# Gate pieces inside the first attention, joined in pairs at fewer places of a step

## The chip, the cores and the metric

The kernel runs on one core of one Trainium2 chip. The metric is the device time of one execution in microseconds. In all views TensorE is PE, its weight loads PEld, VectorE DVE, ScalarE ACT, GpSimd POOL and SyncE SP.

## The reference, cut to what matters

Two transformer blocks run one after the other on 512 tokens of width 1024, in float32. The first block is the one that matters here:

```python
h = rms_norm(x, g_attn[l])
z = h @ w_in[l]
(fq, fk, fv, f_logit, nq, kc, vc, ksl, vsl, kwn, vwn, n_gate, g_a, g_b) = jnp.split(z, offsets, axis=-1)
o_fox = fox_attention(...)      # 8 heads of 64, causal, with a forget bias
o_nsa = nsa_attention(...)      # 8 heads, each a sum of compressed, selected and window attention
merged = jax.nn.sigmoid(g_a) * (o_fox @ w_br_fox[l]) + jax.nn.sigmoid(g_b) * (o_nsa @ w_br_nsa[l])
```

`g_a` and `g_b` are the gates of the two branches: 2048 of the columns of `z`. They are needed only after both attentions, so their matmuls can be run at any time before that.

## The kernel before

**Split operands.** Every large float32 product is made of three matmuls on rounded operands: weights high by activations high, high by low, low by high. ScalarE rounds a weight panel to its high part (`w_hi`, L580 `panel_hi`), VectorE subtracts to get the low part (`w_lo`, L1033 `panel_lo`). A panel is 1024 by 128; a ring of four panel slots is filled by SyncE, and a panel's two parts are made two panels ahead. A panel is eight pieces (k = 0 to 7), a piece three matmuls of 512 columns.

**The first attention.** `inst` lists 32 head instances: eight fox heads, then for each of eight NSA heads a compressed, a selected and a window instance. TensorE's program is written out by hand, software-pipelined over steps s = 0 to 33. In step s it makes the scores of instance s (`qk`, four query tiles t), turns the normalized probabilities of instance s - 2 by transposes (`turn_p`, j = 0 to 3; a compressed instance has one turn of four small transposes), and multiplies them by values (`pv`). Between these calls stand six places, numbered 0 to 5, where `gate_fill(s, slot)` puts a piece of a gate panel if the table `GATE_FILL` has one:

```python
            qk(s, 0)
            qk(s, 1)
            gate_fill(s, 0)
            turn_p(s - 2, 0)
            qk(s, 2)
            gate_fill(s, 1)
            qk(s, 3)
            turn_p(s - 2, 1)
            gate_fill(s, 2)
            pv(s - 2, 0)
            turn_p(s - 2, 2)
            gate_fill(s, 3)
```

Then come `pv(s - 2, 1)`, `turn_p(s - 2, 3)`, place 4, `pv(s - 2, 2)`, place 5 and `pv(s - 2, 3)`.

**The other engines.** VectorE in step s adds the bias to each score tile and takes the row maximum (`score`, L1185), subtracts the high part of each turned tile (`lo_turn`, `pt_lo`, L1219), normalizes instance s - 1 (`normalize`, `factor` L1200 and L1204, then four multiplications, L1210), and at a head's end adds and splits the output (L1235, L1227). ScalarE takes the exponentials (L690), the high part of each turned tile (`pt_hi`, L701), and in fox steps writes the next head's bias into the score buffer (L681). Transposes of instance s - 2 wait for `normed`; product j waits for `pt_lo`; the third score tile of a step waits until VectorE has read the first, since they share a bank.

**Where gate panels end.** All gate panels sum into one bank, `ps[:, 3, :]`. When a panel's last piece is done, VectorE moves it out, scaled, to `gate_z` (`gate_out`, L1244), at the position in its program that belongs to the place (`gate_at`); the next panel's first piece waits for that. The table therefore skips the place after a panel's end. At the end of a step in which a panel ended, ScalarE and VectorE split the panel two ahead (L580, L1033). For gate panels 0 to 7 `gate_out` also waits until the fox keys of a pair are used, since `gate_z` lies over them.

After step 33 the next stage, `branch`, starts on TensorE (L1673) when the last output is split.

## Time and profile before

| | |
|---|---|
| median of 3 runs | 1880.15 us (1878.94 to 1881.78) |
| the profiled execution's own time | 1880.16 us |
| its span in the profile | 1878.3 us |
| TensorE busy, share of the span | 1689.5 us, 90% |
| VectorE busy | 1156.5 us, 62% |
| ScalarE busy | 730.4 us, 39% |
| granted TensorE clock, mean | 0.951 |
| 183 to 424 us: TensorE busy | 215.59 us of 241 |
| 183 to 424 us: VectorE busy | 187.65 us of 241 |

The span is cut into 40 slices of 47 us. The first attention lies in slices 5 to 9. A row of a timeline has start, duration, engine, line, operation, output tile and input tiles, and in brackets how long the engine sat idle before it and what released it. Matmuls are pipelined: a matmul's duration reaches past the start of the next one, so what a matmul costs in a stream is the distance between starts.

### The profile page before, as it was taken

To read this page: it belongs to the slowest core of one execution; us is meant where nothing else is said; L and a number is where in the kernel's file an instruction comes from. 1 tells how busy PE (TensorE), PEld (TensorE's weight loads), DVE (VectorE), ACT (ScalarE), POOL (GpSimd) and SP (SyncE) were. 2 spreads that over 40 slices of the span, in tenths; PEclk is the share of its full clock that TensorE was granted. 3 is DMA by queue.
4 is the path that set the end of the run, shared out by engine and by line. 5 is a ranking of instruction groups with operands and counts; after the bars stand their busy time and mean duration, and the time that the engine had idled before them with its cause. 6 is when DMAs were issued, how large, how long until landed. Compare 5 with 4: busy or idle time off the path is not lost.

```text
span 1878.3 us, 22026 instructions
## 1 busy us (share of the span) xinstructions
PE 1689.5 (90%) x7666; PEld 1354.9 (72%) x7666; DVE 1156.5 (62%) x1741; ACT 730.4 (39%) x1216; POOL 142.5 (8%) x162
## 2 busy tenths in 40 slices
PE   7978889998999999998688867989889699999995
PEld 5867666667888888886566636778667488888884
DVE  6465688875575647465544686768865644354345
ACT  5244775654432323232242234543232344233232
POOL 0001400000000000002000880000000000000000
PEclk9988999998999999998599888999999899999998
DMA  4236821112444444443021110002222123232232
GB/s 154 93 104 185 162 64 46 53 46 76 170 159 166 159 165 160 165 160 131 0 80 55 45 45 0 1 19 94 79 78 90 56 91 100 91 99 95 96 100 79
DMA packets 46983, 178.98 MB, mean 95 GB/s; under 512 B 6256, under 2 KB 6512, under 8 KB 44608
## 3 DMA queue, kind: packets, MB, share of 16 engines
q1 hardware_dynamic: 38304, 136.75, 22.3%
q0 software_dynamic: 8608, 41.29, 7.3%
q8 instruction: 43, 0.70, 0.2%
q14 instruction: 28, 0.23, 0.0%
HBM read 168.04 MB, written 4.73 MB: 92 GB/s over the span
## 4 chain that ended last, share of the span: by engine, by line
PE 63%; DVE 19%; ACT 4%; issue 4%; DVEq 1%; ACTq 0%
PE ps L1673 17%; PE ps L1675 17%; PE ps L1674 17%; DVE conv L1559 3%; PE ps L1939 1%; DVE rstd L1497 1%; PE ps L1876 1%; DVE pt_lo L1522 1%; PE ps L1877 1%; PE ps L1878 1%; PE ps L1837 1%; DVE sq_acc L965 1%; ACT pt_hi L870 1%; DVE w_lo L954 1%; PE ps L1862 1%
## 5 line engine op out<-in xcount | busy, mean ns | idle before, releaser
L1673 PE MATMUL ps<-h_hi,w_hi 128*128 128x512 f32 x1216 | 488.6, 402 | 55.8 <-DVE h_lo L990 15.3
L1674 PE MATMUL ps<-h_lo,w_hi 128*128 128x512 f32 x1216 | 479.1, 394 | 0.0
L1675 PE MATMUL ps<-h_hi,w_lo 128*128 128x512 f32 x1216 | 479.0, 394 | 0.0
L1673 PEld LDWEIGHTS ps<-h_hi,w_hi 128*128 128x128 f32 x1216 | 232.2, 191 | 121.2 <-issue 30.5
L954 DVE TENSOR_TENSOR w_lo<-raw,w_hi 128x1024 fp32r<-128x1024 f32 x196 | 243.5, 1242 | 81.5 <-ACT w_hi L528 69.6
L528 ACT ACTIVATE w_hi<-raw 128x1024 fp32r<-128x1024 f32 x189 | 198.3, 1052 | 238.2 <-DMA raw<-in_panels 236.9
L1674 PEld LDWEIGHTS ps<-h_lo,w_hi 128*128 128x128 f32 x1216 | 232.2, 191 | 49.3 <-issue 2.7
L1675 PEld LDWEIGHTS ps<-h_hi,w_lo 128*128 128x128 f32 x1216 | 231.6, 190 | 49.4
L1673 PE MATMUL ps<-f_hi,w_hi 128*128 128x512 f32 x432 | 171.0, 396 | 0.0
L1675 PE MATMUL ps<-f_hi,w_lo 128*128 128x512 f32 x432 | 170.6, 395 | 0.0
L1674 PE MATMUL ps<-f_lo,w_hi 128*128 128x512 f32 x432 | 170.6, 395 | 0.0
L1673 PEld LDWEIGHTS ps<-f_hi,w_hi 128*128 128x128 f32 x432 | 81.1, 188 | 19.9 <-issue 0.2
L1674 PEld LDWEIGHTS ps<-f_lo,w_hi 128*128 128x128 f32 x432 | 81.1, 188 | 19.8 <-issue 0.2
L1675 PEld LDWEIGHTS ps<-f_hi,w_lo 128*128 128x128 f32 x432 | 81.1, 188 | 19.7
L1033 DVE TENSOR_TENSOR w_lo<-raw,w_hi 128x1024 fp32r<-128x1024 f32 x54 | 65.8, 1221 | 32.5 <-ACT w_hi L580 26.7
L1331 DVE SCALAR_TENSOR_TENSOR X<-ps,mod,X 128x512 f32 (+1 forms) x32 | 24.0, 750 | 98.9 <-PE ps L1675 98.9
L1559 DVE SCALAR_TENSOR_TENSOR conv<-u_pad,vec,conv x96 | 72.1, 751 | 14.4 <-DVE conv L1559 14.4
L701 ACT ACTIVATE pt_hi<-ps 128x512 fp32r<-128x512 f32 (+4 forms) x104 | 46.3, 446 | 73.5 <-PE ps L1837 72.7
L1219 DVE TENSOR_TENSOR pt_lo<-ps,pt_hi 128x512 fp32r<-128x512 f32 (+4 forms) x104 | 52.0, 503 | 34.9 <-ACT pt_hi L701 34.5
L580 ACT ACTIVATE w_hi<-raw 128x1024 fp32r<-128x1024 f32 x61 | 63.7, 1049 | 10.9 <-DMA raw<-in_panels 10.6
L774 ACT ACTIVATE tmp_v<-tmp_s 128x512 f32<-128x512 f32 x32 | 20.2, 633 | 116.2 <-DVE tmp_s L1379 116.2
L1876 PE MATMUL ps<-h_hi,w_hi 128*128 128x512 f32 x128 | 57.0, 445 | 5.7 <-DVE gate_z L1244 5.7
(361 smaller groups left out, 2665.0 us busy)
## 6 DMA issues: line engine op xcount, KB each, us to landing
raw<-in_panels SPq DMA_DIRECT2D x252, 512.0 KB, 3.5
wm<-in_w_mod POOLq DMA_DIRECT2D x16, 1536.0 KB, 10.1
scratch_r<-r POOLq DMA_DIRECT2D x8, 320.0 KB, 9.3
X<-in_x SPq DMA_DIRECT2D x4, 512.0 KB, 7.3
bias<-scratch_c POOLq DMA_DIRECT2D x8, 256.0 KB, 8.9
kd<-k_hi POOLq DMA_DIRECT2D x16, 128.0 KB, 3.6
kd<-k_lo POOLq DMA_DIRECT2D x16, 128.0 KB, 5.2
bias<-scratch_r POOLq DMA_DIRECT2D x8, 256.0 KB, 3.0
```

What stands on the lines that cost most here:

```text
L528: act.activation(w_hi[:, slot], raw[:, slot], ACT.Copy).then_inc(hi_ready, 1)
L580: act.activation(w_hi[:, n % RING], raw[:, n % RING], ACT.Copy).then_inc(hi_ready, 1)
L701: act.activation(pt_hi[0:rows, at:at + w], ps[0:rows, 4 + r % 2, 0:w], ACT.Copy).then_inc(sem("pt_hi_done"), 1)
L954: dve.tensor_tensor(w_lo[:, slot], raw[:, slot], w_hi[:, slot].bitcast(F32), ALU.subtract).then_inc(lo_ready, 1)
L1033: dve.tensor_tensor(w_lo[:, n % RING], raw[:, n % RING], w_hi[:, n % RING].bitcast(F32), ALU.subtract)\
L1219: dve.tensor_tensor(pt_lo[0:rows, at:at + w], ps[0:rows, 4 + r % 2, 0:w], pt_hi[0:rows, at:at + w].bitcast(F32), ALU.subtract).then_inc(se ...
L1331: dve.scalar_tensor_tensor(x, ps[:, u % 2:u % 2 + 1, :], mod[:, bass.ds(i * RING + (gain + u), 1)], x, ALU.mult, ALU.add).then_inc(bank_fr ...
L1559: dve.scalar_tensor_tensor(conv[:, bass.ds(i, 1), :], u_pad[:, bass.ds(i, 1), tap:tap + T], vec[:, bass.ds(i * TAPS + (V_AT["dw_w"] + tap) ...
L1673: pe.matmul(out, w_hi[:, u, b, :], hi[:, k, :N], start=start, stop=False)
L1674: pe.matmul(out, w_hi[:, u, b, :], lo[:, k, :N], start=False, stop=False)
L1675: ins = pe.matmul(out, w_lo[:, u, b, :], hi[:, k, :N], start=False, stop=stop)
L1876: pe.matmul(ps[:, 3, :], hi, h_hi[:, k, :], start=k == 0, stop=False, skip_group_check=True)
```

## The change

`gate_slots` lists fewer places, and each place in `GATE_FILL` now holds two pieces, k and k + 1 of the same panel, run one after the other. The rule that the place after a panel's end is skipped stays, but a place is now two pieces. `gate_fill` loops over the pieces of its place.

```diff
     def gate_slots(s):
 
         if s < 2:
-            return (0, 1, 2, 3, 4, 5)
+            return (0, 2, 3)
         if s >= NI:
-            return (0, 2, 3, 5) if is_big(s - 2) else (0, 2)
+            return (2, 3) if is_big(s - 2) else (2,)
         if is_big(s) and is_big(s - 2):
-            return (0, 1, 2, 3, 5)
-        return (0, 2, 3, 5) if is_big(s - 2) else (0, 1, 2)
+            return (0, 2, 3)
+        return (2, 3) if is_big(s - 2) else (0, 1)
...
             elif _at < 16 * KT:
-                GATE_FILL[s, n] = divmod(_at, KT)
-                _at += 1
+                GATE_FILL[s, n] = [divmod(_at, KT), divmod(_at + 1, KT)]
+                _at += 2
...
-            g, k = GATE_FILL[s, slot]
-            n = BASE["gate"] + g
-            if k == 0:
-                pe.wait_ge(lo_ready, n + 1)
-                pe.wait_ge(bank_free, n + 2)
...
+            for g, k in GATE_FILL[s, slot]:
+                n = BASE["gate"] + g
+                if k == 0:
+                    pe.wait_ge(lo_ready, n + 1)
+                    pe.wait_ge(bank_free, n + 2)
```

What the table says, per kind of step (without the skipped places):

| step s, turned instance s - 2 | before | now |
|---|---|---|
| 0 and 1 | places 0 to 5, one piece | 0, 2, 3, two pieces each |
| fox or selected, large | 0, 1, 2, 3, 5 | 0, 2, 3 |
| window, compressed | 0, 1, 2 | 0, 1 |
| compressed, large | 0, 2, 3, 5 | 2, 3 |
| 32 and 33 | 0, 2, 3, 5 | 2, 3 |

With the skips, the pieces in steps 0 to 2 are 6, 5, 5 before and 6, 4, 6 now; in steps 3 to 8 they are 4, 4, 5, 4, 5, 3 before and 4, 4, 6, 4, 6, 2 now; steps 9 to 31 hold 82 before and 86 now; steps 32 and 33 hold 5 before and none now. Panels end in steps 1, 2, 4, 6, 8, 10, 12, 15, 17, 19, 21, 24, 26, 28, 30, 33 before and in 1, 2, 4, 6, 7, 9, 12, 14, 16, 18, 20, 22, 24, 27, 29, 31 now. Place 5 held a piece in steps 3, 5, 6, 7, 8 and, between 9 and 29, in twelve more; now in none.

**TensorE, step 13 (window), third and fourth scores** (`kn_hi`, `kn_lo` are the keys, `nqs` the queries). Before:

```order
L1817 MATMUL ps<-kn_hi_70,nqs 128x384
L1818 MATMUL ps<-kn_lo_74,nqs 128x384
L1876 MATMUL ps<-h_hi,w_hi 128x512
L1877 MATMUL ps<-h_lo,w_hi 128x512
L1878 MATMUL ps<-h_hi,w_lo 128x512
L1817 MATMUL ps<-kn_hi_70,nqs 128x512
L1818 MATMUL ps<-kn_lo_74,nqs 128x512
L1876 MATMUL ps<-h_hi,w_hi 128x512
L1877 MATMUL ps<-h_lo,w_hi 128x512
L1878 MATMUL ps<-h_hi,w_lo 128x512
```

Now:

```order
L1817 MATMUL ps<-kn_hi_70,nqs 128x384
L1818 MATMUL ps<-kn_lo_74,nqs 128x384
L1876 MATMUL ps<-h_hi,w_hi 128x512
L1877 MATMUL ps<-h_lo,w_hi 128x512
L1878 MATMUL ps<-h_hi,w_lo 128x512
L1876 MATMUL ps<-h_hi,w_hi 128x512
L1877 MATMUL ps<-h_lo,w_hi 128x512
L1878 MATMUL ps<-h_hi,w_lo 128x512
L1817 MATMUL ps<-kn_hi_70,nqs 128x512
L1818 MATMUL ps<-kn_lo_74,nqs 128x512
```

Two pieces stand between the scores in place of one, and the piece behind the fourth score is gone.

**TensorE, from step 13 into step 14 (compressed): products with compressed values `vcs`, first compressed scores, transposes of the selected probabilities `sb`.** Before:

```order
L1862 MATMUL ps<-pt_hi,vcs 128x512
L1863 MATMUL ps<-pt_lo,vcs 128x512
L1817 MATMUL ps<-kc_hi,nqs 128x8
L1818 MATMUL ps<-kc_lo,nqs 128x8
L1817 MATMUL ps<-kc_hi,nqs 128x16
L1818 MATMUL ps<-kc_lo,nqs 128x16
L1876 MATMUL ps<-h_hi,w_hi 128x512
L1877 MATMUL ps<-h_lo,w_hi 128x512
L1878 MATMUL ps<-h_hi,w_lo 128x512
L1837 MATMUL ps<-cst,sb_81 128x128 x4
```

Now:

```order
L1862 MATMUL ps<-pt_hi,vcs 128x512
L1863 MATMUL ps<-pt_lo,vcs 128x512
L1817 MATMUL ps<-kc_hi,nqs 128x8
L1818 MATMUL ps<-kc_lo,nqs 128x8
L1817 MATMUL ps<-kc_hi,nqs 128x16
L1818 MATMUL ps<-kc_lo,nqs 128x16
L1837 MATMUL ps<-cst,sb_81 128x128 x4
```

The piece between the scores and the transposes is gone.

**TensorE, end of step 14: the last transposes and products.** Before:

```order
L1837 MATMUL ps<-cst,sb_81 128x128
L1862 MATMUL ps<-pt_hi,vns 128x256
L1863 MATMUL ps<-pt_lo,vns 128x256
L1876 MATMUL ps<-h_hi,w_hi 128x512
L1877 MATMUL ps<-h_lo,w_hi 128x512
L1878 MATMUL ps<-h_hi,w_lo 128x512
L1862 MATMUL ps<-pt_hi,vns 128x128
L1863 MATMUL ps<-pt_lo,vns 128x128
```

Now:

```order
L1837 MATMUL ps<-cst,sb_81 128x128
L1862 MATMUL ps<-pt_hi,vns 128x256
L1863 MATMUL ps<-pt_lo,vns 128x256
L1862 MATMUL ps<-pt_hi,vns 128x128
L1863 MATMUL ps<-pt_lo,vns 128x128
```

The piece ahead of the last product, at place 5, is gone.

**VectorE, step 1, the scores and the evacuation of the first gate panel:**

```order
 L1185 ISA sb_81,row_max<-ps,sb_81 128x256
 L1185 ISA row_max 128x1
+L1244 TENSOR_TENSOR gate_z_120<-ps,rs_98 128x512
 L1185 ISA sb_81,row_max<-ps,sb_81 128x384
 L1185 ISA row_max 128x1
```

The evacuation now stands ahead of the two large scores; before it stood behind them.

## Rows read from the trace of the kernel before

**Rows 1.** Who waited for whom, 183 to 424 us: us in total, times, longest.

```profile
PE ps L1817 <- DVE row_max L1185: 7.5, 12, 1.3
...
PE ps L1862 <- DVE pt_lo L1219: 6.7, 15, 1.0
...
PE ps L1876 <- DVE gate_z L1244: 5.7, 6, 1.9
```

**Rows 2.** Groups by line and shape, 183 to 424 us, VectorE: busy us, mean ns, idle before.

```profile
L1033 DVE TENSOR_TENSOR w_lo<-raw,w_hi 128x1024 fp32r<-128x1024 f32 x15 | 18.3, 1217 | 0.0
...
L1244 DVE TENSOR_TENSOR gate_z<-ps,rs 128x512 f32<-128x512 f32 x16 | 10.9, 682 | 0.4 <-PE ps L1878 0.4
```

**Rows 3.** Timeline of TensorE, first matmuls of steps 3, 9, 12, 14, 15: start, us.

```profile
208.65 0.27 PE L1817 MATMUL ps<-kd,qs 128*128 128x128 f32 x1
...
259.67 0.27 PE L1817 MATMUL ps<-kn_hi,nqs 128*128 128x128 f32 x1
...
280.83 0.27 PE L1817 MATMUL ps<-kn_hi,nqs 128*128 128x128 f32 x1
...
293.41 0.27 PE L1817 MATMUL ps<-kc_hi,nqs 128*128 128x8 f32 x1
...
300.07 0.27 PE L1817 MATMUL ps<-kn_hi,nqs 128*128 128x128 f32 x1
```

**Rows 4.** Timeline of TensorE, steps 1 and 5; in brackets the idle time before.

```profile
197.43 0.58 PE L1876 MATMUL ps<-h_hi,w_hi 128*128 128x512 f32 x1 [1.87 <-DVE gate_z L1244]
197.81 0.63 PE L1877 MATMUL ps<-h_lo,w_hi 128*128 128x512 f32 x1
198.24 0.63 PE L1878 MATMUL ps<-h_hi,w_lo 128*128 128x512 f32 x1
...
229.24 0.45 PE L1817 MATMUL ps<-kd,qs 128*128 128x384 f32 x1 [1.26 <-DVE row_max L1185]
```

**Rows 5.** Timeline of TensorE, step 12, what follows transposes.

```profile
282.54 0.42 PE L1817 MATMUL ps<-kn_hi,nqs 128*128 128x384 f32 x1
282.80 0.34 PE L1818 MATMUL ps<-kn_lo,nqs 128*128 128x384 f32 x1
...
284.37 0.47 PE L1876 MATMUL ps<-h_hi,w_hi 128*128 128x512 f32 x1
284.69 0.39 PE L1877 MATMUL ps<-h_lo,w_hi 128*128 128x512 f32 x1
```

**Rows 6.** Timeline of TensorE, end of step 12, step 13, start of 14.

```profile
287.85 0.33 PE L1862 MATMUL ps<-pt_hi,vns 128*128 128x128 f32 x1 [0.42 <-DVE pt_lo L1219]
...
289.33 0.60 PE L1834 MATMUL ps<-cst,p_cmp 128*32 128x128 f32 x4
290.35 0.44 PE L1817 MATMUL ps<-kn_hi,nqs 128*128 128x384 f32 x1 [0.42 <-DVE row_max L1185]
...
293.88 0.48 PE L1876 MATMUL ps<-h_hi,w_hi 128*128 128x512 f32 x1
...
294.76 0.66 PE L1837 MATMUL ps<-cst,sb 128*128 128x128 f32 x4
```

**Rows 7.** Timeline of VectorE, step 13.

```profile
291.16 0.67 DVE L1219 TENSOR_TENSOR pt_lo<-ps,pt_hi 32x512 fp32r<-32x512 f32 x1
...
292.23 0.67 DVE L1185 CUSTOM_DVE_ANT_0 sb<-ps,bias 128x512 f32<-128x512 f32 x1
...
293.43 1.27 DVE L1210 TENSOR_SCALAR sb<-sb,factor 128x128 f32<-128x128 f32 x4
```

**Rows 8.** Timeline of TensorE, end of step 14.

```profile
299.17 0.39 PE L1876 MATMUL ps<-h_hi,w_hi 128*128 128x512 f32 x1
...
299.87 0.25 PE L1862 MATMUL ps<-pt_hi,vns 128*128 128x128 f32 x1
```

**Rows 9.** Timeline of TensorE, step 32 and the next stage.

```profile
415.37 0.98 PE L1837 MATMUL ps<-cst,sb 128*128 128x128 f32 x7 [0.39 <-DVE sb L1210]
...
430.81 0.76 PE L1673 MATMUL ps<-qs,w_hi 128*128 128x512 f32 x1 [3.58 <-DVE nqs L1227]
```

More of the change, by code:

```diff
@@ L1869, in gate_fill @@
                 return
-            g, k = GATE_FILL[s, slot]
-            n = BASE["gate"] + g
-            if k == 0:
-                pe.wait_ge(lo_ready, n + 1)
-                pe.wait_ge(bank_free, n + 2)
-            hi, lo = w_hi[:, n % RING, k, :], w_lo[:, n % RING, k, :]
-            pe.matmul(ps[:, 3, :], hi, h_hi[:, k, :], start=k == 0, stop=False, skip_group_check=True)
-            pe.matmul(ps[:, 3, :], hi, h_lo[:, k, :], start=False, stop=False, skip_group_check=True)
-            ins = pe.matmul(ps[:, 3, :], lo, h_hi[:, k, :], start=False, stop=k == KT - 1, skip_group_check=True)
-            if k == KT - 1:
-                ins.then_inc(used, 1)
+            for g, k in GATE_FILL[s, slot]:
[3 more added lines that the diff above has]
+                    pe.wait_ge(bank_free, n + 2)
+                hi, lo = w_hi[:, n % RING, k, :], w_lo[:, n % RING, k, :]
+                pe.matmul(ps[:, 3, :], hi, h_hi[:, k, :], start=k == 0, stop=False, skip_group_check=True)
+                pe.matmul(ps[:, 3, :], hi, h_lo[:, k, :], start=False, stop=False, skip_group_check=True)
+                ins = pe.matmul(ps[:, 3, :], lo, h_hi[:, k, :], start=False, stop=k == KT - 1, skip_group_check=True)
+                if k == KT - 1:
+                    ins.then_inc(used, 1)
         pe.wait_ge(setup, 3)
```

2 lines of the change are left out of this document (1 added, 1 removed).

## The prediction

> **What bounds the kernel now.** I read the 40 slices first: the change touches one stretch, 183 to 431 us, and everything outside it keeps its instructions and their order. Inside, the table of waits [rows 1] shows TensorE stopping for VectorE in three ways: for the release of a score bank (7.5 us in 12 waits), for the low part of a turned probability tile (6.7 us in 15), and, at the first matmul of a gate panel, for the evacuation of the last panel (5.7 us in 6). Then I read the timelines of TensorE and VectorE step by step. Both engines are nearly full there and release each other in turn, so what counts is not the sum of work but which of them is ahead at each hand-over. The same 384 gate matmuls run in both kernels. A gate piece is three matmuls and takes 0.70 us between its neighbours (299.17 to 299.87) [rows 8], a pair 1.40 us. So the time changes only by the waits that pieces cover or leave bare, and by the slow clock.
>
> I call a step by what it scores: fox (0 to 7), then in turn compressed (8, 11, ...), selected (9, 12, ...), window (10, 13, ...). What a step turns and multiplies by values is the step two before.
>
> **1. Start, up to step 3.** Before, TensorE waits 1.87 us at 197.43 for gate_z, which stands on VectorE behind both large scores, and its next matmuls start 0.43 us apart (197.81, 198.24) [rows 4], where the warm ones of a piece take 0.70 us for three [rows 8]: the clock fell to the lower level, 1.2 GHz, after the wait. Now gate_z stands ahead of the two large scores, but for panel 0 it still waits until all keys of fox head 1 are used, so I halve the wait: -0.95. One piece fewer follows it, at 3 x 0.43: -1.3. Step 2 has one piece more, +0.70, and at its end gate_z (0.68) [rows 2] goes ahead of the last low part, where it lies beside ScalarE: -0.65. Sum **-2.2**; bounds -4 (no wait and no slow matmuls) and 0.
>
> **2. Steps 3 to 8,** 51.0 us (208.65 to 259.67) [rows 3]. One piece more: +0.70. The new cost is place 5, the piece between the last two products with values. The last product needs the last turned tile to go through ScalarE and VectorE. With a piece in the gap nothing waits: 299.17, then 299.87 on time [rows 8]. Where the old plan skipped place 5, TensorE stood idle for 0.42 us at 287.85 [rows 6]; with the end of the earlier matmul counted as streamed I take 0.55. Five of these steps had place 5 filled: +2.75. Against it, the pair at place 0 covers 0.70 more of the wait before the third score in steps 5 and 7, of which 1.26 us at 229.24 is the largest [rows 4]: -1.2. Sum **+2.2**; bounds -1 (ScalarE sets the pace of fox steps and hides all) and +4.
>
> **3. Steps 9 to 32, up to the transposes of step 32,** 155.7 us (259.67 to 415.37) [rows 3, 9]. I build it from the read triple 12 to 14, 280.83 to 300.07, 19.24 us with 11 pieces [rows 3].
> With all places full it now has 14 pieces: +2.10.
> The wait at 290.35 (0.42 idle, 0.67 from the end of streaming) goes, since the pair at place 0 outlasts the split w_lo (1.22 us) [rows 2, 6]: -0.67. The pair at place 2 covers another 0.2 before a first product.
> The place-5 wait, paid once in this triple (287.85), is now paid twice: +0.58.
> The large term is the compressed step. Its first transposes need the normalized tile. In step 13 the order is: compressed transposes from 289.33, pt_lo at 291.16, the largest score at 292.23, normalizing at 293.43 for 1.27, transposes at 294.76 [rows 6, 7]: 2.53 us from largest score to transposes, which no piece can shorten. Three things used to fill TensorE meanwhile: pieces at places 1 and 2 of the window step and place 0 of the compressed one (293.88). Now one pair, at place 1, which stands before the fourth score. TensorE has 0.70 us less to do, and the matmuls of the largest score end 0.70 later after those transposes; of that I let VectorE's own queue ahead of it (pt_lo and the third score) hide 0.15, so the largest score starts 0.55 late. So a wait of about 0.1 becomes 1.4: +1.30.
> Full triple: 19.24 + 2.10 - 0.87 + 0.58 + 1.30 = 22.35. Steps 9 to 31 are eight selected, eight window and seven compressed steps: eight triples less one compressed step (8.3, by the same walk), plus the 1.4 of step 32: 8 x 22.35 - 8.3 + 1.4 = 171.9. That holds 108 pieces; the plan puts 86 there, because eleven pairs are skipped for evacuations: 22 x 0.70 = -15.4. A skipped pair bares what it covered. By the walk that is 0.1 to 0.5 where place 2 or 3 of a selected or place 3 of a compressed step is skipped, 1.0 at place 0 of a window step behind w_lo, and 1.5 to 2.1 where gate_z falls ahead of the normalizing of a compressed turn (steps 16, 22, 31). Mean 0.8, eleven times: +8.8. Result 165.3, so **+9.6**. Of this 4 x 0.70 = 2.8 is pieces that step 9 to 31 take over from the last steps. Bounds: if the compressed wait stayed at 0.1 and no hole cost anything, 165.3 - 8.8 - 10.4 = 146.1, -9.6; if each hole cost the full 2.1, +24. I take the walk, which is nearest to the read triple.
>
> **4. Tail,** 415.37 to 430.81 [rows 9]. Five pieces lay here, all beside waits; taking them out saves nothing. But gate_z (0.68) and one w_lo (1.22) [rows 2] leave VectorE's last chain, of which the first counts whole and the second for what stands behind ScalarE's copy: **-1.1**, bounds -1.9 and 0.
>
> Nothing else moves: DMA issues keep their order on both queues; kd and bias loads follow the score steps. The joined piece should cost nothing by itself. After transposes the next matmul starts late: 284.37 to 284.69 is 0.32 where a streamed one takes 0.23. But the score matmul of 384 columns behind transposes shows the same, 282.54 to 282.80, 0.26 [rows 5], so the loss moves with the transposes and is not saved. The Trainium skill (TensorE: Matmul & The Clock Gate, step-by-step on LDWEIGHTS) says that the next weights load while the current matmul runs, which speaks for long runs; by that alone each of 64 joins would gain. The trace prices such a join at most 0.08, 5.1 us in all, and shows it paid elsewhere.
>
> Sum: -2.2 + 2.2 + 9.6 - 1.1 = +8.5. On the profiled execution's own 1880.16 us, which is the median of the runs shown (1880.15) to 0.01, this gives 1888.7; I say **1889**.
>
> **Rivals.** *Faster.* The covers win: the score and evacuation waits (7.5 + 5.7) go, and the compressed steps do not get a longer wait, because VectorE, no longer held by TensorE's late transposes, runs ahead by as much as the pair is long. It decides at one point: the transposes of the compressed steps start less than 0.5 us after TensorE is ready. Place 5 still costs 0.42 in 18 steps, 7.6. 1880.2 - 13.2 + 7.6 = 1874.6. For it: the read waits are real, and VectorE idles where TensorE is busy. Against: the 2.53 us chain in [rows 7] has no gap in it.
> *No change.* VectorE's own work per triple is unchanged, and if it is the true pace the loss at place 0 is given back at the next hand-over: +9.6 shrinks to about +2, 1881.
> *Worse.* The boundaries (gate_z 0.68 and w_lo 1.22, fifteen times [rows 2]) stay as exposed as now instead of lying under pairs: another 0.5 each, 7.5, 1896. The long waits of steps 17 and 32 could also bring the low clock, as at 197.43; if nine matmuls then run at 0.43 instead of 0.23, that is 1.8 us more each time. The Trainium skill (same page, what's actually happening) says that activity releases the throttle; the granted clock after 197.43 agrees.
> *The joins pay.* Rule above, with place 5 and holes as walked: 1889 - 5.1 = 1883.6.
>
> **How the numbers follow.** The runs shown lie within 0.15% of each other, and I call 0.2% (3.8 us) what can be told from no change: 1876.4 to 1883.9. Chances: forecast (1884 to 1893) 0.53, faster 0.16, no change 0.13, worse 0.14, joins 0.04. Slower by over 0.2%: 0.53 + 0.14 = 0.67; within 0.2%: 0.13 + 0.04 = 0.17; faster 0.16. The range 1876 to 1898 leaves out the faster case and the far end of the worse one, nearly 0.2. The forecast's own range is 1884 to 1893.
>
> **What would show it.** After: no TensorE wait for gate_z, or under 1.5 us in all; the waits for the score bank about halved; the waits of the last product for pt_lo at almost every step, some 20 times 0.4; the waits of compressed-step transposes for the normalized tile at 1.2 to 1.5 us eight times, some 10 us; step 9 starting within 1 us of 259.7; the next stage starting about 8 us later than 430.8. I am wrong if step 9 starts several us earlier, or if transposes in compressed steps wait under 0.5 us.

## The result, and the profile after

| | before | after |
|---|---|---|
| median | 1880.91 us (1878.94 to 1881.78, 4 runs) | 1912.38 us (1907.90 to 1916.11, 4 runs) |
| the profiled execution's own time | 1880.16 us | 1915.98 us |
| its span in the profile | 1878.3 us | 1914.2 us |
| mean granted TensorE clock | 0.951 | 0.938 |

The change makes the kernel slower by 31.5 us, a ratio of 1.0168 (95% interval 1.0137 to 1.0198). 1889 us was forecast, with 1898 as the upper end. The direction was right; the loss is almost four times the 8.5 us forecast.

I read the windows first, cut at the same instructions in both kernels: the stage from its first waiting matmul to the first matmul of `branch`. Columns: stretch, its length, busy time of PE, PEld, DVE, ACT and POOL (with instructions), granted clock, share of DMA, GB/s. Before:

```profile
181.12:430.81 249.69, 220.32 (x1164) 170.04 (x1165) 193.12 (x651) 159.09 (x444) 24.98 (x46) 0.96 0.32 77
259.67:415.37 155.70, 141.53 (x753) 107.38 (x753) 128.50 (x463) 94.34 (x285) 3.95 (x7) 0.99 0.15 49
```

After, the whole stage, and steps 9 to 32 up to the transposes of step 32:

```profile
182.69:461.34 278.65, 234.94 (x1165) 186.40 (x1165) 193.63 (x651) 158.79 (x444) 25.04 (x46) 0.90 0.30 69
263.34:444.68 181.34, 153.92 (x763) 121.42 (x762) 129.64 (x465) 94.89 (x286) 3.95 (x7) 0.92 0.14 45
```

The stage takes 278.65 us for 249.69, 29.0 more. VectorE and ScalarE do the same work in the same busy time. TensorE runs the same matmuls (1164 and 1165 records), but is busy 14.6 us longer (220.32 to 234.94), and idle 14.3 us longer (29.37 to 43.71). **Half of the loss is waiting, half is matmuls at a lower clock**: the granted clock of the stage falls from 0.96 to 0.90. Of the rest of this execution's 35.8 us, 1.57 lie ahead of the stage and 5.4 in later stages (1452.9 for 1447.5 us), whose instructions did not change; another run of the same table of pieces (e10 below) has 1447.5 there, so these 5.4 are no part of the change.

The other executions say the same. Each has its own mean granted clock on record: 0.943 and 0.942 for the changed kernel's executions of 1907.9 and 1908.8 us, 0.939 and 0.938 for those of 1916.1 and 1916.0. Their mean is 0.9405, that of the 68 executions of the kernel before that were timed beside the experiments 0.9515. Within either kernel an execution is longer by 1.7 or 1.8 us for each 0.001 of clock that it has less, over all kernels of this case by 1.5. The 0.011 between the two is then worth, by estimate, 16 to 20 us of the 31.5; the rest is waiting.

The waits, after, which answer to [rows 1] (waiting line, what it waited for, us in total, times, longest):

```profile
PE ps L1862 <- DVE pt_lo L1219: 17.3, 32, 2.0
PE ps L1837 <- DVE sb L1210: 16.1, 12, 2.7
PE ps L1817 <- DVE row_max L1185: 5.2, 9, 1.3
...
PE ps L1876 <- DVE gate_z L1244: 1.3, 1, 1.3
```

The waits for gate_z are nearly gone, as meant (5.7 in six before, 1.3 in one now). Those for the score bank went from 7.5 to 5.2. In their place, waits of products for `pt_lo` (6.7 in 15 before) and of first transposes for the normalized tile grew to 33.4 us in 44. Eighteen of the former stand ahead of a step's last product with nothing at place 5, seventeen of them 0.45 or 0.46 us long and one 0.26. The latter, in steps that score a compressed tile, look like this, here in step 20 (columns: start, duration, engine, line, operation, output and inputs, form, count, idle time before it and what ended it):

```profile
350.70 0.66 PE L1837 MATMUL ps<-cst,sb 128*128 128x128 f32 x4 [1.38 <-DVE sb L1210]
...
352.18 0.39 PE L1877 MATMUL ps<-h_lo,w_hi 128*128 128x512 f32 x1
```

Five such waits are 1.38 us. Where a panel ends in the window step ahead, the wait is longer. VectorE and TensorE at the end of step 16 and in step 17:

```profile
322.95 0.68 DVE L1219 TENSOR_TENSOR pt_lo<-ps,pt_hi 32x512 fp32r<-32x512 f32 x1 [1.02 <-ACT pt_hi L701]
323.56 0.67 DVE L1244 TENSOR_TENSOR gate_z<-ps,rs 128x512 f32<-128x512 f32 x1
324.16 0.54 DVE L1185 CUSTOM_DVE_ANT_0 sb<-ps,bias 128x384 f32<-128x384 f32 x1
...
324.63 0.67 DVE L1185 CUSTOM_DVE_ANT_0 sb<-ps,bias 128x512 f32<-128x512 f32 x1
...
325.83 1.27 DVE L1210 TENSOR_SCALAR sb<-sb,factor 128x128 f32<-128x128 f32 x4
```

```profile
323.78 0.47 PE L1862 MATMUL ps<-pt_hi,vcs 32*128 32x512 f32 x1 [0.67 <-DVE pt_lo L1219]
...
327.16 1.11 PE L1837 MATMUL ps<-cst,sb 128*128 128x128 f32 x4 [2.14 <-DVE sb L1210]
...
329.91 0.63 PE L1877 MATMUL ps<-h_lo,w_hi 128*128 128x512 f32 x1
```

`gate_z` (323.56) stands in VectorE's chain from pt_lo to the normalizing, and the chain has no gap; TensorE meanwhile has no piece to run, since the place behind a panel's end is skipped, and stands 2.14 us. After that a gate matmul takes 0.43 us to its neighbour where at 352.18 it takes 0.23: the lower level of 1.2 GHz. Step 10 shows the two losses side by side:

```profile
274.67 0.61 PE L1817 MATMUL ps<-kn_hi,nqs 128*128 128x384 f32 x1 [1.32 <-DVE row_max L1185]
...
275.39 0.63 PE L1876 MATMUL ps<-h_hi,w_hi 128*128 128x512 f32 x1
...
277.52 0.63 PE L1878 MATMUL ps<-h_hi,w_lo 128*128 128x512 f32 x1
```

```profile
278.74 0.69 DVE L1185 CUSTOM_DVE_ANT_0 sb<-ps,bias 128x512 f32<-128x512 f32 x1 [1.87 <-PE ps L1818]
...
279.95 1.27 DVE L1210 TENSOR_SCALAR sb<-sb,factor 128x128 f32<-128x128 f32 x4
```

```profile
281.28 0.33 PE L1837 MATMUL ps<-cst,sb 128*128 128x128 f32 x1 [1.38 <-DVE sb L1210]
```

A wait of 1.32 us for the score bank; then the pair at place 1 runs at 1.2 GHz, 2.56 us (275.39 to 277.95) for 1.40; VectorE waits 1.87 us for the largest score behind it; the normalizing begins at 279.95; the transposes wait 1.38 us. VectorE is late by what TensorE is late, so nothing of the slow pair is won back. It does not make the next wait longer either: behind window step 19, which ran at the full clock, the transposes of step 20 wait the same 1.38 us.

### The profile page after: what moved, and what is told of

Read it like the earlier page. It is cut to its first block, busy times and chain, and to the rows that moved or that the text cites. A ratio compares the mean times of both kernels' runs of the same rounds, so it can differ in the third digit from the quotient of the medians.

```text
span 1914.2 us, 22026 instructions
## 1 busy us (share of the span) xinstructions
PE 1710.5 (89%) x7666; PEld 1376.4 (72%) x7666; DVE 1157.4 (60%) x1741; ACT 730.4 (38%) x1216; POOL 143.6 (8%) x162
## 4 chain that ended last, share of the span: by engine, by line
PE 63%; DVE 18%; ACT 5%; issue 4%; DVEq 1%; ACTq 0%
PE ps L1673 17%; PE ps L1674 16%; PE ps L1675 16%; DVE conv L1559 3%; PE ps L1876 2%; PE ps L1878 1%; PE ps L1877 1%; PE ps L1939 1%; DVE rstd L1497 1%; PE ps L1837 1%; DVE pt_lo L1522 1%; DVE sb L1210 1%; DVE sq_acc L965 1%; PE ps L1862 1%; DVE w_lo L954 1%
## 5 line engine op out<-in xcount | busy, mean ns | idle before, releaser
L1673 PE MATMUL ps<-h_hi,w_hi 128*128 128x512 f32 x1216 | 491.6, 404 | 54.8 <-DVE h_lo L990 15.5
L1033 DVE TENSOR_TENSOR w_lo<-raw,w_hi 128x1024 fp32r<-128x1024 f32 x54 | 65.8, 1221 | 31.5 <-ACT w_hi L580 25.8
L774 ACT ACTIVATE tmp_v<-tmp_s 128x512 f32<-128x512 f32 x32 | 20.3, 633 | 116.4 <-DVE tmp_s L1379 116.4
L1837 PE MATMUL ps<-cst,sb 128*128 128x128 f32 x240 | 46.9, 299 | 16.1 <-DVE sb L1210 16.1
```

The lines of the kernel that those rows point to most:

```text
L1033: dve.tensor_tensor(w_lo[:, n % RING], raw[:, n % RING], w_hi[:, n % RING].bitcast(F32), ALU.subtract)\
L1673: pe.matmul(out, w_hi[:, u, b, :], hi[:, k, :N], start=start, stop=False)
L1837: ins = pe.transpose(ps[:, 4 + r % 2, (t - j) * P:(t - j + 1) * P], sb[big_of[s]][:, SB_AT[t] + j * P:SB_AT[t] + (j + 1) * P], ident)
```

## The experiments

Every run was timed against the kernel before on the same chip; ratios are to it, with 95% intervals. The kernel before had medians of 1880.5 (e1 to e4), 1880.5 (e5 to e8), 1881.0 (e9 to e12) and 1883.0 us (e13 to e15) beside them; the numbers are those of the runs' labels, given with each heading. In the diffs (place, pieces) is an entry of the table. "Busy" and "idle" are TensorE's in the stage of one profiled execution, to be read beside 220.32 and 29.37 us in the kernel before and 234.94 and 43.71 in the changed one.

### Undoing one part at a time

**e2: Place 5 filled again.** In the changed kernel, half of the pair at place 3 goes to place 5:

```diff
+        three = ((3, 1), (5, 1))
...
-            return (0, 2, 3)
-        return (2, 3) if is_big(s - 2) else (0, 1)
+            return ((0, 2), (2, 2), *three)
+        return ((2, 2), *three) if is_big(s - 2) else ((0, 2), (1, 2))
```

> The changed kernel with the pair at place 3 split into one piece at place 3 and one at place 5 (from step 2 on), otherwise paired as it is. Theory: a bare place 5 costs 0.46 to 0.58 us; about 18 of them are filled again, so 8 to 10 us go, and with less idle time some of the low clock: 1898 to 1904. Rival (the transposes of the compressed steps are the whole cause): the waits at place 5 only move to the next hand-over, 1909 to 1913.

Measured: 1904.45 us (1899.83 to 1909.16), ratio 1.0113 [1.0080, 1.0147], 7.9 us less than the changed kernel, the lower end of the 8 to 10 that the waits add up to. Of low clock nothing is gone: the mean clock of its four executions is that of the changed kernel, 0.9405. The rival (1909 to 1913) does not hold by the time. In the profiled execution, the longest of the four, the waits for `pt_lo` fell from 17.3 to 10.2 us and TensorE is idle for 5.7 us less (37.98); some of it did come back, in waits of first transposes (17.5 for 16.1 for the normalized tile). That profile has more low clock than the changed kernel's (busy 237.94), so its stage is only 2.7 us shorter.

**e3: The compressed steps covered.** The window steps' pair at place 1 moves to place 0 of the compressed steps:

```diff
-        return (2, 3) if is_big(s - 2) else (0, 1)
+        return (0, 2, 3) if is_big(s - 2) else (0,)
```

> The changed kernel with the pair at place 1 of the window steps (ahead of the fourth score) moved to place 0 of the steps that score a compressed tile (ahead of the transposes that wait 1.38 us). Theory: the largest score is 1.4 us earlier and a pair fills the wait, so 8 waits of 1.38 to 2.7 (14.1 us in the profile) fall under 0.3; with them goes the low clock that follows the longest: 12 us of waits and some 8 of slow matmuls, 1890 to 1896. Place 5 stays bare. Rival (VectorE's own chain sets the pace there, what one wait loses another gains): 1906 to 1912.

Measured: 1899.96 us (1896.99 to 1903.58), ratio 1.0104 [1.0075, 1.0133], 12.4 us less. The waits, up to the end of the stage:

```profile
PE ps L1862 <- DVE pt_lo L1219: 19.3, 38, 0.8
PE ps L1837 <- DVE sb L1210: 7.3, 7, 2.2
PE ps L1817 <- DVE row_max L1185: 5.8, 12, 0.7
```

Waits for the normalized tile fell from 16.1 us in 12 to 7.3 in 7. (The eight longest had added up to 13.7 us, not 14.1.) The waits gained less than forecast because the pair left place 1 of the window steps: with neither place 1 nor 2 filled the product of the compressed tile waits, as here in step 16,

```profile
316.48 0.46 PE L1862 MATMUL ps<-pt_hi,vcs 32*128 32x512 f32 x1 [0.79 <-DVE pt_lo L1219]
```

and where a panel ends in the window step, place 0 behind it is skipped and the full wait remains (2.15 us at 363.20, in step 23). So idle time fell by only 5.9 us (37.80), and busy time by 8.2 (226.70), the stage clock being 0.94 for 0.90. The larger part of this gain is clock, in the four executions too: their mean is 0.9465 for 0.9405, worth 9 to 11 of the 12.4 us by the estimate above.

**e14: Both at once.**

```diff
+        three = ((3, 1), (5, 1))
...
-            return (0, 2, 3)
-        return (2, 3) if is_big(s - 2) else (0, 1)
+            return ((0, 2), (2, 2), *three)
+        return ((0, 2), (2, 2), *three) if is_big(s - 2) else ((0, 2),)
```

> The changed kernel with both parts undone at once: place 5 filled with half of the pair of place 3, and the window steps' second pair moved to place 0 of the compressed steps. Alone they took 8 and 12.4 us off. Theory (separate waits, separate prices): together 20, 1892; what is left are the bare place 2 of the window steps (8 waits of 0.67 = 5.4), and that the pieces are used up by step 29, so the last steps have none. 1889 to 1895. Rival (both take off the same low clock): less than the sum, 1896 to 1900.

Measured: 1893.30 us (1892.49 to 1899.15), ratio 1.0056 [1.0040, 1.0071]. That is 19.1 us less than the changed kernel (21 by the ratios, as this chip ran the kernel before 2 us slower), for 7.9 + 12.4 = 20.3 alone. The two prices add up, and so does the idle time of the profiles: 5.7 and 5.9 us less alone, 10.5 together (33.24). That speaks for separate waits, but it is not a clean test. All three plans place other numbers of pieces per step than the changed kernel, so panels end elsewhere in them. In this one three panels end at place 0 of a window step; place 0 of the compressed step behind it is skipped, and waits of 2.14 or 2.15 us for the normalized tile are left in steps 14, 20 and 26, each with a low clock behind it (0.68 or 0.69 over the step). Of the 10 us that still separate this run from the kernel before, its executions' clock (0.942 for 0.951 on that chip) can make up all.

### The same question from the kernel before

**e12: One joining alone, place 5 to place 3**, in the fifteen steps that have both; order and panels stay:

```diff
+        if s >= 2 and (s, 3) in GATE_FILL and (s, 5) in GATE_FILL:
+            GATE_FILL[s, 3] = GATE_FILL[s, 3] + GATE_FILL.pop((s, 5))
```

> The kernel before with the other joining alone: the piece at place 5 stands at place 3 behind the one there, in the fifteen steps that have both, from step 2 on; nothing else moves. Theory: each place 5 left bare costs 0.46 to 0.58 us, and few of the waits are long enough to bring the low clock: +7 to +9, 1888 to 1890. Rival 1 (what place 5 loses, the pair at place 3 wins back): 1881 to 1883. Rival 2 (many short waits bring the low clock too): 1893 or more.

Measured: 1893.85 us (1889.48 to 1895.96), ratio 1.0071 [1.0058, 1.0085]. The profiled execution was the shortest, 1889.48, and in it the stage is only 7.5 us longer (257.14), at a clock of 0.98 (0.96 before):

```profile
182.75:439.89 257.14, 221.41 (x1164) 171.41 (x1165) 193.29 (x651) 159.14 (x444) 24.99 (x46) 0.98 0.31 75
```

```profile
303.42 0.33 PE L1868 MATMUL ps<-pt_hi,vns 128*128 128x128 f32 x1 [0.46 <-DVE pt_lo L1225]
```

The fifteen waits are 0.46 us each as expected; with the earlier matmul's end counted as streamed, 0.5 to 0.6. Of the profiled execution's 9.3 us, 7.5 lie in the stage and 1.6 ahead of it, where nothing was changed. Nor is it free of low clock: steps 3 and 20 ran at 0.84 and 0.83, where the kernel before has 1.00, and took 1.2 and 1.6 us more than there, while steps 0 and 1, the same in both, took 2.5 less. The median is 4.4 us above the profiled execution, and its number is rival 2's, not the theory's. The five executions' clocks go with their times: 0.953 for 1889.5 us, 0.950 and 0.951 for 1892.7 and 1893.9, 0.948 for 1895.7 and 1896.0. The next run asks whether the clock makes the difference.

**e15: The same with the wait filled**, by one gate matmul run twice:

```diff
+            if (s, 5) not in GATE_FILL and s >= 2 and is_big(s - 2):
+                repeat()
```

> The kernel before with the piece of place 5 joined to place 3, as run already (median 1893.9, profile 1889.5), with one gate matmul (512 columns, hi x hi of the last piece, while its panel is open) run again in each bare place 5: 0.23 us of work in a wait of 0.46. (The gate values are changed by the repeated products.) Theory: the waits' ends stay, 9.3 us; the low clock that came on top in the median (some 4 us) is less: 1889 to 1891. Rival 1 (the clock has no part in it): 1893 to 1894.5. Rival 2 (the repeated matmul delays the last product): 1896.

Measured: 1889.44 us (1888.04 to 1893.56) beside 1882.97, ratio 1.0040 [1.0025, 1.0055]; without the fill it was 1.0071 [1.0058, 1.0085]. The intervals do not touch. Step for step the profile has the same lengths as the run without the fill, within 0.1 us, so the fill moved no wait's end. About 0.3% went, and of what was tried only the clock accounts for it. The two profiles, both with a stage clock of 0.98, do not show it themselves, but the executions do: 0.951 to 0.954 here, 0.948 to 0.953 without the fill. The median is the theory's; the first rival would have left the ratio, the second raised it.

**e11: The other joining alone, place 1 to place 0**, in eleven fox and selected steps:

```diff
+        if s >= 2 and is_big(s) and is_big(s - 2) and (s, 0) in GATE_FILL and (s, 1) in GATE_FILL:
+            GATE_FILL[s, 0] = GATE_FILL[s, 0] + GATE_FILL.pop((s, 1))
```

> The kernel before with one joining alone: in fox and selected steps from step 2 on, the piece at place 1 stands at place 0 behind the one there (eleven pairs); number, order and panels of all pieces unchanged. Theory (pairs cost nothing, bare places do): place 1 has no wait to cover and the pair at place 0 outlasts some waits for the score bank, so 1878 to 1881. Rival (joining itself costs, say 0.5 us a pair): 1886.

Measured: 1880.22 us (1876.56 to 1882.62), ratio 0.9994 [0.9985, 1.0003]. A pair as such costs nothing that these runs can tell. This run and e12 both join pieces; e12 bares a wait by it and this one does not.

### Clock or wait

**e1: Small matmuls in the bare waits** of the changed kernel, n = 9 ahead of the transposes in compressed steps and 3 at place 5:

```diff
+        def idle_fill(n):
+            for _ in range(n):
+                pe.matmul(ps[:, 2, 3 * P:4 * P], cst_r[:, 0:P], cst_r[:, P:2 * P], start=True, stop=True,
+                          skip_group_check=True)
...
+            if kind_of(s) == "cmp" or s == NI:
+                idle_fill(9)
...
+            if is_big(s - 2) and s > 8:
+                idle_fill(3)
```

> The changed kernel with matmuls added that compute nothing that is used (9 of 128 columns before the first transposes of each step that scores a compressed tile, and of step 32; 3 before the last product with values, from step 9 on). They write a part of a score bank that nothing reads. At 0.11 us each they last 1.0 us in waits of 1.38 and 0.33 in waits of 0.46, so the waits' ends do not move. Theory (two factors, waits and the low clock they bring): the ends of the waits stay, but TensorE no longer stands idle, the granted clock of 264 to 448 us rises from 0.91 to 0.97 or more, and most of the 14.6 us by which the stage's matmuls run longer goes: 1898 to 1902. Rival (waits alone make the loss, the clock is a detail of one profile): 1912, or some us more for the added work, 1912 to 1916.

Measured: 1906.29 us (1899.40 to 1912.57), ratio 1.0122 [1.0079, 1.0164]. By the median 6 us less, but the interval overlaps that of the changed kernel. The profiled execution speaks against an effect: step 17 and the whole stretch are as before the fill,

```profile
322.69 0.47 PE L1862 MATMUL ps<-pt_hi,vcs 32*128 32x512 f32 x1 [0.67 <-DVE pt_lo L1219]
...
323.79 1.20 PE L1884 MATMUL ps<-cst_r 128*128 128x128 f32 x9
326.07 1.11 PE L1837 MATMUL ps<-cst,sb 128*128 128x128 f32 x4 [1.08 <-DVE sb L1210]
...
328.82 0.63 PE L1877 MATMUL ps<-h_lo,w_hi 128*128 128x512 f32 x1
```

```profile
262.24:443.73 181.49, 166.27 (x879) 134.72 (x879) 129.67 (x465) 94.92 (x286) 3.96 (x7) 0.92 0.14 45
324.00:325.00 1.00, 0.99 (x9) 0.85 (x8) 0.90 (x7) 0.95 (x3) 0.48 (x1) 0.98 0.00 0
325.00:326.00 1.00, 0.00 (x0) 0.00 (x0) 1.00 (x5) 0.75 (x4) 0.07 (x1) 0.50 0.42 53
```

181.49 us at a clock of 0.92 (181.34 and 0.92 in the changed kernel). TensorE ran without a gap from 323.79 to 324.99, and the clock fell right behind it: 0.98 in the slice up to 325, 0.50 in the next. In this execution the small matmuls did not keep the clock. But the profile was taken of one of two long executions (1911.2 and 1912.6 us, clock 0.942 and 0.941); the other two took 1899.4 and 1901.4 us at 0.949 and 0.948, a clock that none of the changed kernel's four reached (0.938 to 0.943), and their times are in the theory's range. So this run leaves open whether the small matmuls did something in half of the executions. Next come matmuls of a gate piece's size.

**e5: Gate-size matmuls in the same places:**

```diff
+                    pe.matmul(ps[:, 3, :], w_hi[:, (BASE["gate"] + g) % RING, k, :], h_hi[:, k, :],
+                              start=False, stop=False, skip_group_check=True)
...
+            if kind_of(s) == "cmp" or s == NI:
+                repeat(5)
...
+            if kind_of(s - 2) == "cmp":
+                repeat(2)
...
+            if is_big(s - 2) and s > 8:
+                repeat(1)
```

> The changed kernel with matmuls of a gate piece's own size (512 columns) in the bare places: the hi x hi matmul of the piece that ran last is run again, one ahead of the last product, two ahead of the first product that follows transposes of a compressed tile, five ahead of the transposes in steps that score a compressed tile, and in step 32. (While no gate panel is open, small matmuls that nothing reads stand in their place, none at the second of the three. The gate values come out changed by the repeated products; no other part differs.) They take 0.23, 0.46 and 1.15 us in waits of 0.46, 0.67 and 1.38 or more. Theory: the clock followed the full-size pieces that are missing there, so it stays up, and most of the 14.6 us of slower matmuls goes: 1898 to 1903, the waits' ends unmoved. Rival 1 (after the run with small matmuls): the low clock does not depend on these waits, the same stretches run slow, 1906 to 1912. Rival 2: added work is on the path: above 1912.

Measured: 1904.28 us (1902.80 to 1906.91), ratio 1.0109 [1.0072, 1.0146]; 8.1 us less than the changed kernel. In its profile:

```profile
181.12:449.81 268.69, 239.57 (x1264) 191.63 (x1265) 193.40 (x651) 158.72 (x444) 24.93 (x46) 0.95 0.30 71
260.05:432.65 172.60, 158.20 (x849) 125.67 (x848) 129.32 (x465) 94.88 (x285) 3.95 (x7) 0.98 0.14 47
```

```profile
317.50 1.31 PE L1875 MATMUL ps<-cst_r 128*128 128x128 f32 x10
319.79 0.80 PE L1837 MATMUL ps<-cst,sb 128*128 128x128 f32 x4 [0.98 <-DVE sb L1210]
...
322.22 0.63 PE L1890 MATMUL ps<-h_lo,w_hi 128*128 128x512 f32 x1
```

The stage takes 268.7 us, 10.0 less than in the changed kernel, though it runs 99 matmuls more; steps 9 to 32 take 172.60 for 181.34, and their clock is 0.98. The 8.7 us are clock, or nearly: at the full clock in both profiles, the fill makes window steps 13, 19 and 28 0.4 to 0.5 us longer and compressed steps 20 and 29 0.3 to 0.4 shorter, which nearly cancels. In steps 17 and 23, where no panel was open and small matmuls stood in again, the low clock stayed; in the others of steps 10 to 31 where the changed kernel's profile has it, it is gone. All four executions have a clock of 0.946 to 0.950, above all four of the changed kernel, and none of their times reaches the changed kernel's shortest. Beside e1 the time alone proves nothing (1904.3 and 1906.3 us); that matmuls of this size did more than small ones rests on the two profiles, steps 17 and 23 and the executions' clocks. The median shows less than the 9 to 14 us I had expected; this profile's later stages have 7.8 us more than the kernel before (1455.3 for 1447.5), as the changed kernel's profile has 5.4.

### Where in the stage, and the panels' ends

**e4: Pairs in steps 0 to 8 only** (old entries from step 9):

```diff
+        if s < 9:
+            if s < 2 or is_big(s):
+                return ((0, 2), (2, 2), (3, 2))
+            return ((2, 2), (3, 2))
```

> Pairs only in steps 0 to 8, the old single pieces and places from step 9 on. Theory by the sum on record: -2.2 at the start, +2.2 in steps 3 to 8, so 1881 within 2 us; as the trace of the changed kernel shows step 8 alone 2.4 us longer, up to 1883. Rival (pairs cost about the same in every step, 30 us over 32 steps): 1888.

Measured: 1887.57 us (1884.51 to 1892.32), ratio 1.0033 [1.0021, 1.0046], the rival's value. But the profile puts only 3.2 us ahead of step 9, and 7.6 behind it, where the entries are the old ones: by step 8 the pairs have placed one piece more, so that all later panels end one place sooner. And nearly all of these 10.8 us are slower matmuls, not waits: busy 230.60, idle 29.86, the stage clock 0.92 for 0.96. Two runs take this apart.

**e6: The same with one piece fewer in step 8**, so that nothing slips:

```diff
+        if s < 8:
+            return ((0, 2), (2, 2), (3, 2)) if s < 2 or is_big(s) else ((2, 2), (3, 2))
+        if s == 8:
+            return ((2, 2), (3, 1))
```

> As the run with pairs in steps 0 to 8 alone, with one piece fewer in step 8 (one at place 3, for two), so that from step 9 on every piece and every panel end stands exactly where the kernel before has it. Theory: in that run the 8.2 us that steps 9 to 30 took longer came from the panel ends, which one piece more had moved (steps 15 and 24 took 12.2 and 10.3 for 7.8); here they are back, so only the change of the first nine steps is left: 3 us longer by the start of step 9, 1882 to 1885. Rival (a slip of one piece costs nothing, the difference comes from another cause): 1887 to 1888 again.

**e7: The slip alone**, no pairs:

```diff
+        if s == 8:
+            return ((0, 1), (2, 1), (3, 1), (5, 2))
```

> The kernel before with one piece more in step 8 (two at place 5) and otherwise its own places: all later panel ends come one place earlier, nothing is paired. Theory: the place of the panel ends has a price of its own, about that of steps 9 to 30 in the run with pairs in steps 0 to 8: +8 in the profile less what the median gave, 1884 to 1889. Rival: 1881 within 2 us.

Measured: e6 1883.84 us (1881.62 to 1889.99), ratio 1.0011 [0.9995, 1.0028], and e7 1883.91 us (1882.30 to 1892.72), 1.0018 [0.9999, 1.0037]. Both medians lie over 3 us above the kernel before, near what the theories say, and together make about the 7 us of the run above; but neither interval excludes no change. In e6's profile the stage is 4.1 us longer, all of it busy time (224.45) at an unchanged idle time (29.34); steps 8, 9 and 20 ran at a low clock. So what e6 prices is where low clock fell, not waits. What the slip does to the waits is plain in e7's profile: step 15 takes 10.9 us for 7.8. A panel now ends at place 5 of step 14 and `gate_z` stands ahead of the normalizing; idle before matmuls in that step goes from 0.95 to 2.37 us, and the rest is low clock behind it (0.84 over the step, 1.00 before):

```profile
301.41 0.44 PE L1840 MATMUL ps<-cst,sb 128*128 128x128 f32 x2 [1.68 <-DVE sb L1213]
```

**e8: Old pieces in steps 0 to 8, pairs behind them:**

```diff
+        if s == 8:
+            return ((0, 1), (2, 1), (3, 1), (5, 2))
+        if s > 8:
...
+            if is_big(s) and is_big(s - 2):
+                return ((0, 2), (2, 2), (3, 2))
+            return ((2, 2), (3, 2)) if is_big(s - 2) else ((0, 2), (1, 2))
```

> Old places and single pieces in steps 0 to 8 (with the one piece more in step 8), pairs from step 9 on exactly as in the changed kernel. Theory: the loss lies here: the 25.6 us of steps 9 to 32 and the tail's 1.2 stay, the first nine steps' are back: 1906 to 1910. Rival (the early waits set off the later ones, without them the later steps run as walked, +9.6): 1888 to 1893.

Measured: 1905.96 us (1900.82 to 1912.31), ratio 1.0120 [1.0074, 1.0166]. It has the slip too, so 22 us stand against the run with the slip alone; in the profiles of the two, 13.0 us are busy time (235.12 for 222.11) and 11.0 idle (42.28 for 31.30). The loss lies from step 9 on; the rival's +9.6 is excluded.

**e10: gate_z off the chain.** In the changed kernel, in window steps:

```diff
-            gate_at(s, 0)
+            if kind_of(s) != "win":
+                gate_at(s, 0)
...
-            gate_at(s, 1)
+            if kind_of(s) != "win":
+                gate_at(s, 1)
...
             normalize(s - 1)
+            if kind_of(s) == "win":
+                gate_at(s, 0, 1)
```

> The changed kernel with one order of VectorE changed: in window steps the evacuation of a panel (gate_z, 0.67 us) stands behind the normalizing instead of ahead of the third score or behind the fourth. That is so in steps 16, 22, 25 or 31 where a panel ends at place 0 or 1. Theory: gate_z is on the chain to the transposes of the next step, so these waits (2.14 at step 17, 1.99 at step 23, 2.69 at step 32) fall by 0.5 to 0.7 each to the 1.38 of the other compressed steps, about 2 us, and the low clock behind them with it: 1904 to 1910. Rival (the chain there is ScalarE's, gate_z lies beside it): the waits stay within 0.2, 1912.

Measured: 1912.91 us (1912.75 to 1912.96, 3 runs), ratio 1.0169 [1.0153, 1.0185]. No gain, the rival's time; but not by its mechanism. The waits did fall, each by 0.6 (to 1.54, 1.38 and 2.09 us), and step 17 is 0.3 us shorter (11.34 for 11.67). In step 23 the next one grew by as much:

```profile
378.15 0.80 PE L1862 MATMUL ps<-pt_hi,vns 128*128 128x512 f32 x1 [1.35 <-DVE pt_lo L1219]
```

```profile
379.07 0.80 PE L1866 MATMUL ps<-pt_hi,vns 128*128 128x512 f32 x1 [1.95 <-DVE pt_lo L1219]
```

And the low clock came in places where the changed kernel, with the same waits, did not have it. Step 20 in this run, to be read beside 350.70 and 352.18 above:

```profile
350.28 1.12 PE L1841 MATMUL ps<-cst,sb 128*128 128x128 f32 x4 [1.39 <-DVE sb L1210]
...
353.03 0.63 PE L1881 MATMUL ps<-h_lo,w_hi 128*128 128x512 f32 x1
```

The same wait (1.39 and 1.38 us), the same instructions; here the matmuls are 0.43 apart and the step takes 11.21 us, there 0.23 and 8.28. Step 21 is the other way round, 8.96 us here at the full clock and 10.53 at 0.84 there, and the clocks of the three executions (0.939 each) are within those of the changed kernel.

### Using what costs nothing

**e9: Pairs in steps 0 to 3 only.** Both plans have placed 20 pieces by then, so nothing slips:

```diff
+        if s < 4:
+            return ((0, 2), (2, 2), (3, 2))
```

> The changed plan (pairs at places 0, 2, 3) in steps 0 to 3 only; from step 4 on every piece and panel end exactly as before. Both plans have placed 20 pieces by then, so nothing slips. Theory: from the first score to step 4 the kernel before took 36.0 us and the changed one 34.0; the later steps start from the same state, so 2 us less: 1878 to 1879.5. Rival: the gain is given back by the next steps (VectorE, whose work is the same, is no earlier): 1880 to 1882.

Measured: 1880.31 us (1878.32 to 1882.75), ratio 0.9999 [0.9990, 1.0008], the rival's value. In the profile the way to step 4 is 2.3 us shorter (33.7 for 36.0) and stays so to step 11 (87.9 for 90.2). Step 11 then takes 10.79 us for 8.62, at a low clock, behind the same waits (0.66 and 0.58 us, for 0.65 and 0.57).

**e13: This and place 1 joined to place 0:**

```diff
+        if s < 4:
+            return ((0, 2), (2, 2), (3, 2))
...
+        if s >= 4 and is_big(s) and is_big(s - 2) and (s, 0) in GATE_FILL and (s, 1) in GATE_FILL:
+            GATE_FILL[s, 0] = GATE_FILL[s, 0] + GATE_FILL.pop((s, 1))
```

> Both joinings that cost nothing alone: the changed plan in steps 0 to 3, and from step 4 on the piece of place 1 joined to place 0 in fox and selected steps; everything else as before. Theory: in the profiles the first shortened the way to step 4 by 2.0 us, the second that from step 9 to 31 by 1.3, and both medians lay 0.7 us under the kernel before; together 1878 to 1880 (-1 to -3). Rival: both gains are only where low-clock stretches happened to fall, 1881.

Measured: 1878.42 us (1876.58 to 1883.24, 11 runs) beside 1882.97 (15 runs), ratio 0.9979 [0.9969, 0.9988]. It is the only version that beats the kernel before, by 0.2%, and it beats the changed one. Its waits up to 424 us, against [rows 1]:

```profile
PE ps L1868 <- DVE pt_lo L1225: 8.9, 19, 1.1
PE ps L1882 <- DVE gate_z L1250: 5.2, 6, 1.3
PE ps L1823 <- DVE row_max L1191: 4.0, 10, 0.7
PE ps L1843 <- DVE sb L1216: 3.2, 8, 0.6
```

For the score bank 4.0 us, where it was 7.5.

## Why the prediction was right and wrong

**Term 1, start to step 3, -2.2: right.** From the first score to step 3 the profile gives 25.05 us for 26.68, -1.6; the wait for gate_z is 1.31 for 1.87. Pairs in steps 0 to 3 alone show it again (2.3 us by step 4).

**Term 2, steps 3 to 8, +2.2: low by 1.5, nearly all of it clock.** Measured 54.75 for 51.02, +3.7. Step 8 alone takes 9.62 for 7.26: a panel now ends at place 3 of step 7, its `gate_z` (252.33) and `w_lo` (254.70) stand ahead of step 8's scores on VectorE, and the first product of that step, at 258.29, waits 2.04 us where it waited 0.96. I had no row for that in this term. But step 8 also ran at a clock of 0.82; in e5's profile, with the same pieces (and small matmuls ahead of its transposes) and the full clock, it takes 8.32 us, and steps 3 to 8 together 53.44, +2.4. There the way from the first score to step 9 is 78.10 us for 77.70 before: terms 1 and 2, which add up to nothing, hold apart from the clock.

**Term 3, steps 9 to 32, +9.6: this step failed; it measured +25.6.** Its parts did not fail alike.

- *The full triple* held. Steps with all places filled and the full clock take 8.94 us (selected, steps 15 and 30), 5.28 (window, step 19) and 8.28 (compressed, step 20), 22.5 in all, where the walk had 22.35; selected steps 9 and 24, in which a panel ends at place 3, take 8.5. The wait of the first transposes was walked as 1.4 and measured 1.38; place 5 at 0.58 measured 0.46 of bare idle, and 7.9 us when filled again.
- *The clock* was missing from the sum, and is the larger part. 8.7 us of these steps went in the run with gate-size matmuls, and steps 17 and 23 kept a clock of 0.84 there, which leaves up to 3.4 more: 9 to 12 of the 16.0 us. I had put the low clock only beside the rival "worse", twice 1.8 us, and took it there for a matter of the longest waits. Step 10 shows it behind a wait of 1.32, step 20 of e10 behind one of 1.39.
- *The holes* were mis-sized, by 4 to 7 us together with the rest of the walk. I took eleven skipped pairs as saving 15.4 and costing 8.8 (0.8 each). With nearly all low clock gone (e5, clock 0.98 for 0.99 before) these steps take 172.6 us where the sum had 165.3. If the 7.3 between were all holes, each would cost 1.5, a little more than the pair it saves (1.40); with the 3.4 of clock taken off it is 1.2. Steps at the full clock show where: a skipped place 2 or 3 costs what the walk had (selected steps 7.94 and 7.35 us for 8.94, compressed step 29 7.31 for 8.28, so a cost of 0.4 or less of the 1.40), a skipped place 1 of window step 16 too (4.59 us for 5.28, and 0.76 more wait behind it, 1.5 in all for the 1.5 walked). A skipped place 0 saves nothing: step 25 takes 5.27 for 5.28 (cost 1.4, walked as 1.0), step 21 takes 8.95 in e5 and 8.96 in e10 for 8.94 (cost 1.4, no price in the walk). The longest waits of the steps behind window steps 16, 22 and 31 (2.14, 1.99, 2.69 us) are 0.8, 0.6 and 1.3 over the ordinary 1.38. Moving gate_z off that chain took 0.6 off each wait, but not off the time.

**Term 4, tail, -1.1: wrong sign.** 16.66 us for 15.44, +1.2. The granted clock there was 0.52, for 0.86 before (windows of the two kernels from the transposes of step 32). Taking out the pieces "beside waits" did save no waiting, as the term said. The 1.1 us that the evacuation and the split should have given back did not show, and the low clock stands beside that; that the pieces had kept the clock is likely, but no run put full-size matmuls there (in step 32 of e5 only small ones could run, and its tail takes 17.16 us at 0.60).

**The joins** cost nothing that can be told from no change: 0.9994 [0.9985, 1.0003] for eleven of them. The rival's 0.08 each, 0.9 us in eleven, is too small for this run to exclude.

**The signs named beforehand.** gate_z under 1.5 us: yes. Some twenty waits of 0.4 at place 5: yes, eighteen. Eight waits of 1.2 to 1.5 us before transposes of compressed steps: there, three of them longer. Score waits halved: no, 5.2 for 7.5. Step 9 within 1 us of 259.7: no, 263.34, of which 1.57 lies ahead of the stage. The next stage 8 us later: no, 30.5.

**The rivals.** The faster case named its own point of decision, transposes waiting under 0.5 us; they waited 1.38. "No change" supposed that VectorE's pace gives back what a bare wait takes; e12 speaks against it, where fifteen waits of 0.46 us, bared alone, make the stage 7.5 us longer. The worse one was nearest, with one of the two causes named but priced at twice 1.8 us (the clock), and the other (place 0 skipped) not.

What decides whether a given wait brings the low clock stays open: e10 and e9 show that the same waits sometimes bring it and sometimes not. The split of the median's 31.5 us into clock (16 to 20) and waiting is an estimate from the executions' clocks, in agreement with the one profile (14.6 and 14.3 of the stage's 29.0).

## What to carry to other kernels

Price a removed filler by the wait that it leaves bare on the engine, and then ask a second question of every bare wait: does the busy engine's clock survive it? Where an engine hands over to another in turn, spread its free work over all hand-overs rather than in fewer, larger portions; here joining was free only where the place that was emptied had no wait. Compare the granted clock of every execution, not of the profiled one alone. And when a table places work with a fixed cycle of skips, one piece more or less shifts every later boundary: hold the phase fixed before comparing two plans, which e2, e3 and e14 did not.

## What the runs showed of the hardware that was not expected

- In one profiled execution, nine matmuls of 128 columns without a gap (1.20 us) in a wait did not keep the clock: steps 9 to 32 stayed at 0.92. In another, with gate-size ones (512 columns) in the same places, it was 0.98, and these steps took 8.7 us less with more matmuls in them. Single executions of the first kernel had a mean clock of 0.941, 0.942, 0.948 and 0.949, of the second 0.946 to 0.950, of the kernel without any fill 0.938 to 0.943.
- The same wait is followed by the low clock in one execution and not in another: 1.38 us in step 20 with matmuls 0.23 apart, 1.39 us with 0.43. The Trainium skill (TensorE: Matmul & The Clock Gate, What's actually happening) says that the number of slow matmuls at the start of one kernel varies from run to run. The like is seen here in mid-kernel, between two kernels with the same instructions in that step.
- Later stages, whose code did not change, took 5.4 and 7.8 us more in two profiles than in that of the kernel before. A difference of a few us between two single profiles is read stage by stage.
